# A two-layer decoder step on one core: three expert slots in turn through the whole loop, an early read of the overflow flag, and layer 1's keys transposed ahead of the last sums

## The reference

```python
group = argmax(hf @ wg + bg)                      # 4 groups
top_val, top_idx = top_k(exp_logits[group], 2)    # 2 of 8 experts in the group
gate = p_group * softmax(top_val)
for each of 32 experts e, on the rows that chose it:
    gu = xb @ w_up[e]                             # 1024 -> 2 x 512
    rows = (silu(gu[:, :512]) * gu[:, 512:]) @ w_down[e]
y[token] += rows * gate
```

## Time and profile before

| | |
|---|---|
| time, median of 3 runs | 1537.93 us (1533.36 to 1538.13) |
| profiled execution, its own time | 1538.02 us |
| its span, first to last instruction | 1536.4 us |
| mean granted TensorE clock | 0.957 |
| busy: PE / PEld / DVE / ACT / POOL | 1401.6 / 680.5 / 484.9 / 274.7 / 127.4 us |
| expert loop of layer 0 / of layer 1 | about 366 to 822 us / 1062 to 1518 us |
| read from HBM | 455.72 MB |

### The profile page before, as it was taken

How to read it: one execution, slowest core, us unless ns; L and a number is a source line. 1 busy time by engine, 2 the same in 40 slices (tenths; PEclk the granted TensorE clock), 3 DMA queues, 4 the chain that set the end, 5 groups by cost and what they waited for, 6 DMA issues and landing times.

```text
span 1536.4 us, 30978 instructions
## 1 busy us (share of the span) xinstructions
PE 1401.6 (91%) x13378; PEld 680.5 (44%) x13378; DVE 484.9 (32%) x1257; ACT 274.7 (18%) x748; POOL 127.4 (8%) x179
## 2 busy tenths in 40 slices
PE   7999998487999999999997599987999999999996
PEld 4477898344333333333333465744333333333332
DVE  3647375424122122122122425334122122122122
ACT  3214232201111111111112222110111111111111
POOL 3000586000000000000001010100000000000000
PEclk9999999798999999999998698998999999999998
DMA  9622300468799999999997345258799999999994
GB/s 338 192 83 48 78 4 4 120 274 328 317 396 428 426 430 429 429 428 428 429 426 246 116 103 173 95 203 358 318 392 428 427 428 428 430 429 427 427 428 179
DMA packets 69910, 463.63 MB, mean 302 GB/s; under 512 B 12002, under 2 KB 32732, under 8 KB 45052
## 3 DMA queue, kind: packets, MB, share of 16 engines
q1 hardware_dynamic: 68172, 456.00, 73.2%
q0 software_dynamic: 1648, 6.33, 1.5%
HBM read 455.72 MB, written 6.59 MB: 301 GB/s over the span
## 4 chain that ended last, share of the span: by engine, by line
PE 88%; DVE 7%; ACT 2%; issue 2%; POOL 0%; DMA 0%; POOLq 0%; DVEq 0%; SPq 0%; ACTq 0%
PE bank L1208 31%; PE bank L1194 12%; PE bank L751 10%; PE bank L1221 8%; PE bank L993 6%; PE bank L1272 4%; PE bank L910 4%; PE bank L1055 2%; PE bank L1201 2%; DVE arena L1773 2%; PE bank L928 1%; PE bank L801 1%; PE bank L897 1%; PE bank L721 1%; PE bank L860 1%
## 5 line engine op out<-in xcount | busy, mean ns | idle before, releaser
L1208 PE MATMUL bank<-slot,arena 128*32 128x256 f32 x3968 | 477.7, 631 | 1.0 <-DVE arena L1776 1.0
L1208 PEld LDWEIGHTS bank<-slot,arena 128*32 128x32 f32 x3968 | 137.7, 123 | 268.4 <-issue 252.9
L1194 PE MATMUL bank<-h,arena 128*32 128x256 f32 x1536 | 190.8, 640 | 1.2 <-DVE arena L1769 1.2
L1781 DVE SCALAR_TENSOR_TENSOR arena<-arena,bank 128x128 f32<-128x128 f32 x64 | 18.5, 289 | 366.7 <-ACT arena L1404 365.0
L1221 PE MATMUL bank<-slot,arena 128*32 128x256 f32 x1984 | 119.9, 382 | 0.7 <-ACT arena L1408 0.7
L1417 ACT COPY arena<-bank 32x256 f32<-32x256 f32 x252 | 91.4, 363 | 152.9 <-PE bank L1221 150.7
L1194 PEld LDWEIGHTS bank<-h,arena 128*32 128x32 f32 x1536 | 63.4, 129 | 113.2 <-issue 111.8
L1404 ACT ACTIVATE arena<-bank 128x128 f32<-128x128 f32 x64 | 17.8, 278 | 452.8 <-PE bank L1208 452.8
L565 POOL TENSOR_SCALAR arena<-arena 128x1 f32<-128x1 f32 (+2 forms) x18 | 5.8, 320 | 1054.6 <-ACT h L1392 1014.4
L2172 DVE TENSOR_TENSOR x<-bank,x 128x512 f32<-128x512 f32 x64 | 44.1, 691 | 138.3 <-PE bank L1272 138.0
L1272 PE MATMUL bank<-arena 128*128 128x512 f32 x128 | 73.6, 663 | 6.0 <-issue 6.0
(11 more groups left out here) (399 smaller groups left out, 1415.2 us busy)
## 6 DMA issues: line engine op xcount, KB each, us to landing
slot<-in_exp_w_up SPq DMA_DIRECT2D x124, 2048.0 KB, 15.9
slot<-in_exp_w_down SPq DMA_DIRECT2D x62, 2048.0 KB, 16.1
slot<-in_w_in SPq DMA_DIRECT2D x6, 1536.0 KB, 7.4
slot<-in_w_out SPq DMA_DIRECT2D x4, 2048.0 KB, 8.7
arena<-in_exp_w_up SPq DMA_DIRECT2D x2, 4096.0 KB, 26.8
slot<-in_w_in SPq DMA_DIRECT2D x3, 2048.0 KB, 8.1
slot<-in_w_in SPq DMA_DIRECT2D x5, 1024.0 KB, 11.1
slot<-in_w_mem_kv SPq DMA_DIRECT2D x2, 2048.0 KB, 13.6
```

The lines of the kernel that those rows point to most:

```text
L1194: last = pe.matmul(ps[0][strip * CAP:(strip + 1) * CAP, 0:DW], G[:, t, :], h[:, t, :].rearrange("p (f k) -> p k f", k=KT)[:, strip * (DW / ...
L1208: last = pe.matmul(ps[bank][strip * CAP:(strip + 1) * CAP, 0:2 * FW], xs[:, c, strip_k * CAP:(strip_k + 1) * CAP], up_cols(wup[slot_j], k, ...
```

## The change

Experts use the three slots in turn through the whole loop: expert e goes to slot e mod 3, and its load waits for expert e - 3. Since four experts make a quad and three slots a turn, TensorE's loop body becomes three quads (12 experts), run twice; VectorE's and ScalarE's loops stay at one quad, SP's takes three experts. The down part of the third slot is two DMAs. PE, ACT and DVE read the overflow flag behind the first quad; the `If` stays behind the last. TensorE transposes layer 1's keys behind the `If` of layer 0 and ahead of the last sums. Expert 30 is now in slot 0 and expert 31 in slot 1, so KC is loaded when expert 30 is done, then the two chunks when expert 31's up part is done, then VC. `select(1)` moves behind the norm's scales, since its place belongs to the third slot until then.

```diff
+RING = 3
+LOADS = [len(range(j, NE, RING)) for j in range(RING)]
@@ load_down
-            sp.dma_start(wdn[sl], A["exp_w_down"][l, bass.ds(e, 1)].rearrange("e (p k) n -> p (e k) n", p=128)).then_inc(sem, 16)
+            w = A["exp_w_down"][l, bass.ds(e, 1)].rearrange("e (p k) n -> p (e k) n", p=128)
+            if sl < THIRD:
+                sp.dma_start(wdn[sl], w).then_inc(sem, 16)
+            else:
+                for u in range(2):
+                    sp.dma_start(wdn_third[u], w[:, 2 * u:2 * u + 2, :]).then_inc(sem, 16)
@@ SP
+            def load_cache(l, name, to, sem):
+                for m in range(2):
+                    sp.dma_start(to[:, m], A[name][l].rearrange("b (m p) h d -> m p b (h d)", p=128)[m]).then_inc(s[sem], 16)
...
-                refill(3, 0, 0)
-                refill(4, 1, 1)
-                with sp.Fori(2, NE // 2 - 1) as i:
-                    refill(2 * i + 1, 0, 2 * i - 1)
-                    refill(2 * i + 2, 1, 2 * i)
-                refill(NE - 1, 0, NE - 3)
+                with sp.Fori(1, NE // RING) as i:
+                    for j in range(RING):
+                        refill(RING * i + j, j, RING * i + j - RING)
+                for e in range(NE // RING * RING, NE):
+                    refill(e, e % RING, e - RING)
                 if l == 0:
                     sp.wait_ge(s["m_used"], UNITS * (NE - 1))
+                    load_cache(1, "cache_mem_k", KC, "cache_k")
+                    sp.wait_ge(s["m_used"], UNITS * (NE - 1) + UNITS_UP)
                     for n in range(2):
                         load_w_in(1, n)
+                    load_cache(1, "cache_mem_v", VC, "cache_v")
@@ POOL
                 norm_scale(2 * l + 2)
-                if l == 0:
-                    pool.wait_ge(s["m_used"], UNITS * 3)
-                    select(1).then_inc(s["consts"], 1)
...
                 norm_scale(2 * l + 3)
+                if l == 0:
+                    select(1).then_inc(s["consts"], 1)
@@ PE
                 if l == 0:
                     memory0()
-                else:
-                    keys_T(1)
                 attention(l)
...
-                expert(0, 0, 0, loads[0] + 16, started=l > 0)
-                expert(1, 1, 1, loads[1] + 16, started=l > 0)
-                expert(2, THIRD, 0, 16 * (l + 1), between=places_between(0, l == 0))
-                expert(3, 0, 1, loads[0] + 32)
-                with pe.Fori(1, QUADS - 1) as g:
-                    expert(4 * g, 1, 0, loads[1] + 32 * g, between=sum_between(g - 1))
-                    expert(4 * g + 1, 0, 1, loads[0] + 32 * g + 16)
-                    expert(4 * g + 2, 1, 0, loads[1] + 32 * g + 16, between=places_between(g))
-                    expert(4 * g + 3, 0, 1, loads[0] + 32 * g + 32)
-                g = QUADS - 1
...
+                def quad(g, c, turn, places_first=False, sums=True, final=False):
+                    for j in range(4):
+                        sl = (c + j) % RING
+                        between = lambda k: None
+                        if j == 0 and sums:
+                            between = sum_between(g - 1)
+                        if j == 2:
+                            between = places_between(g, places_first)
+                        expert(4 * g + j, sl, j % 2, 16 * (LOADS[sl] * l + 1) + 16 * (turn + (c + j) // RING),
+                               started=sums or j >= 2 or l > 0, final=final and j == 3, between=between)
+                quad(0, 0, 0, places_first=l == 0, sums=False)
                 pe.wait_ge(s["flag"], l + 1)
                 more = pe.value_load(flag_i[0:1, 0:1], min_val=0, max_val=1)
+                with pe.Fori(0, 2) as i:
+                    for n in range(3):
+                        quad(3 * i + n + 1, 4 * (n + 1), 4 * i)
+                quad(QUADS - 1, 4 * (QUADS - 1), 0, final=True)
                 r = lambda n: s[f"r_{n}{l}"]
                 with pe.If(more > 0):
...
                 with pe.Else():
                     pe.nop()
+                if l == 0:
+                    keys_T(1)
                 pe.wait_ge(s["m_S4T"], QUADS * (l + 1))
@@ ACT, and DVE alike
                 quad(0, first=l == 0)
+                act.wait_ge(s["flag"], l + 1)
+                more = act.value_load(flag_i[0:1, 0:1], min_val=0, max_val=1)
                 with act.Fori(1, QUADS - 1) as g:
                     quad(g)
                 quad(QUADS - 1, final=True)
-                act.wait_ge(s["flag"], l + 1)
-                more = act.value_load(flag_i[0:1, 0:1], min_val=0, max_val=1)
```

More of the change, by code:

```diff
@@ L424, in _ @@
                     sp.dma_start(ga2[0:16, :], A["gla_a2"][0]).then_inc(s["lora_in"], 16)
-                for m in range(2):
-                    sp.dma_start(KC[:, m], A["cache_mem_k"][l].rearrange("b (m p) h d -> m p b (h d)", p=128)[m]).then_inc(s["cache_k"], 16)
-                    sp.dma_start(VC[:, m], A["cache_mem_v"][l].rearrange("b (m p) h d -> m p b (h d)", p=128)[m]).then_inc(s["cache_v"], 16)
+                if l == 0:
+                    load_cache(0, "cache_mem_k", KC, "cache_k")
+                    load_cache(0, "cache_mem_v", VC, "cache_v")
                 if l == 0:
@@ L466, in _ @@
                 load_down(sp, 1, 1, l, s["wdn1"])
-                sp.dma_start(wdn_third[1], third_down[:, 2:4, :]).then_inc(s["wdn_third"], 16)
+                sp.dma_start(wdn_third[1], third_down[:, 2:4, :]).then_inc(s["wdn2"], 16)
                 sp.wait_ge(s["norm_h"], 6 * (l + 1))
@@ L471, in _ @@
                 sp.wait_ge(s["logit_ps"], 3 * (l + 1))
-                sp.dma_start(wdn_third[0], third_down[:, 0:2, :]).then_inc(s["wdn_third"], 16)
+                sp.dma_start(wdn_third[0], third_down[:, 0:2, :]).then_inc(s["wdn2"], 16)
                 def refill(e, j, after):
@@ L496, in _ @@
                     sp.wait_ge(s["m_used"], UNITS * NE * (l + 1))
-                    load_up(sp, 0, 0, l, (s[f"rw{l}"],) * 2)
-                    load_down(sp, 0, 0, l, s[f"rw{l}"])
+                    load_up(sp, 0, THIRD, l, (s[f"rw{l}"],) * 2)
+                    load_down(sp, 0, THIRD, l, s[f"rw{l}"])
                     with sp.Fori(1, NE) as e:
                         sp.wait_ge(s[f"r_pe{l}"], len(REST["pe"]) * STEPS_REST * e)
-                        load_up(sp, e, 0, l, (s[f"rw{l}"],) * 2)
-                        load_down(sp, e, 0, l, s[f"rw{l}"])
+                        load_up(sp, e, THIRD, l, (s[f"rw{l}"],) * 2)
+                        load_down(sp, e, THIRD, l, s[f"rw{l}"])
                 with sp.Else():
@@ L1304, in expert @@
                     for k in range(KT):
[L1305 to L1307 removed]
+                        if k % (KT // 2) == 0:
                             pe.wait_ge(s[f"wup{'ab'[k // (KT // 2)]}{sl}"], loaded)
@@ L1321, in expert @@
                         pe.wait_ge(s["m_nat"], it - 1)
-                    if sl == THIRD:
-                        pe.wait_ge(s["wdn_third"], 2 * loaded)
-                    else:
-                        pe.wait_ge(s[f"wdn{sl}"], loaded)
+                    pe.wait_ge(s[f"wdn{sl}"], 2 * loaded if sl == THIRD else loaded)
                     for f in range(FF // 128):
                         down_f(sl, f, 6 + par).then_inc(s["m_used"], 1)
-                loads = [16 * (NE // 2) * l, 16 * (NE // 2 - 1) * l]
@@ L1339, in _ @@
-                g = QUADS - 1
-                expert(4 * g, 1, 0, loads[1] + 32 * g, between=sum_between(g - 1))
-                expert(4 * g + 1, 0, 1, loads[0] + 32 * g + 16)
-                expert(4 * g + 2, 1, 0, loads[1] + 32 * g + 16, between=places_between(g))
-                expert(4 * g + 3, 0, 1, loads[0] + 32 * g + 32, final=True)
+                def quad(g, c, turn, places_first=False, sums=True, final=False):
[8 more added lines that the diff above has]
+                               started=sums or j >= 2 or l > 0, final=final and j == 3, between=between)
@@ L1349, in _ @@
                     with pe.Fori(0, NE) as e:
-                        pe.wait_ge(s[f"rw{l}"], 48 * (e + 1))
+                        pe.wait_ge(s[f"rw{l}"], 64 * (e + 1))
                         for b in range(STEPS_REST):
@@ L1359, in _ @@
                             for k in range(KT):
-                                last = up_k(0, k, 2)
+                                last = up_k(THIRD, k, 2)
                             last.then_inc(r("pe"), 1)
@@ L1365, in _ @@
                             for f in range(FF // 128):
-                                last = down_f(0, f, 6)
+                                last = down_f(THIRD, f, 6)
                             last.then_inc(r("pe"), 1)
@@ L2205, in _ @@
                 quad(0, first=True)
+                dve.wait_ge(s["flag"], l + 1)
+                more = dve.value_load(flag_i[0:1, 0:1], min_val=0, max_val=1)
                 with dve.Fori(1, QUADS - 1) as g:
@@ L2212, in _ @@
                 last.then_inc(s["m_nat_dve"], 1)
-                dve.wait_ge(s["flag"], l + 1)
```

(1 more changed line is left out.)

7 lines of the change are left out of this document (2 added, 5 removed).

## The result

The changed kernel takes 1549.86 us (median of 7 runs, 1546.71 to 1555.79), the kernel before 1537.93 us beside it: a ratio of 1.0087, interval 1.0063 to 1.0111. The forecast was 1541.8 us in a range of 1534 to 1547: it had the sign, and a third of the size. By the prediction's own bounds this is slower, to which it gave 0.42.

What follows compares the result with a forecast made beforehand. The prediction took TensorE's pace to bound the expert loops. Flag -0.9 - 0.7 + 0.4, keys -2.0 and two jumps back +7.0 gave +3.8 us on 1538.0, so 1541.8 us, range 1534 to 1547.

Steps and rivals of the forecast that it cites:

- The bound and the third slot: Expert loops: they run at TensorE's pace with weights in time, so a third buffer removes no wait; gain 0.
- three quads aren't held: TensorE's jump from loop end to head: three quads of code exceed what the engine holds, so it takes 3.54 us.
- The price of the edge: One taken jump back in each layer's TensorE loop: 3.5 us, +7.0 for two, bounds 0 to 14.6.
- The second fetch: Behind the loop's jump back: a second instruction packet may be waited for, 0 to 3.5 us, taken as 0.3.
- the clock's term: TensorE behind the loop's jump back: 0.6 us, chosen between 0 and 1.2.
- The jump in layer 0: Jump past the overflow part, ahead of the last sums: it stays, at 3.54 us, and TensorE waits for it.
- The flag: Flag read leaves the loop's end: -0.9 and -0.7 us; at its new place behind the fourth expert +0.4 in all.
- The keys: Layer 0's end, keys transposed ahead of the last sums: -2.0 us, bounds -2.6 and -1.0.
- the second: Loop's jump back waits for two fetches and for the clock, 14.6 us in all: 1549.4 us; chance 0.08.
- Rival 1: Loop's jump back stays free, its code held or fetched ahead: not slower, 1534.8 us; chance 0.17.
- rival 3: Expert loops: weights are the bound after all and deeper loading lets TensorE run closer: 1534.1 us; chance 0.06.
- rival 4: Flag and keys gain nothing, being hidden already; only jumps back and new reads count: 1545.4 us; chance 0.09.

Runs made afterwards that it cites:

- numbers 4: Kernel before with only TensorE's loop body grown to three quads, run twice, with two slots and loads as they were: 1551.85 us, ratio 1.0089.
- 11: Kernel before with early flag, keys ahead, TensorE's overflow body as a loop (short jump), layer 1's two projection loads behind the jump: 1526.91 us, ratio 0.9945.
- number 2: Changed kernel with layer 1's first loads held back until TensorE's key transposes, behind its jump past the overflow part: 1545.41 us, ratio 1.0063.
- number 3: Changed kernel with weight refills cut to 128 KB a half, so most experts compute with old weights: one run of 1553.63 us.
- number 1: Changed kernel with TensorE's six inner quads written out, so that it jumps back nowhere: 1535.93 us, ratio 0.9994.
- experiment 5: Kernel before with only the flag read early and layer 1's keys transposed ahead of the last sums: 1532.88 us, ratio 0.9967.
- number 8: Kernel before with TensorE's loop body of two quads, run three times a layer, buffers and loads as before: one run of 1561.13 us.
- number 6: Changed kernel with TensorE's inner quads written out and layer 1's first loads issued behind the jump past the overflow part: 1531.94 us, ratio 0.9952.
- number 7: The kernel of number 6 with TensorE's overflow body as a loop over its eight steps, so the jump past it is short: 1527.54 us, ratio 0.9929.
- numbers 9: Changed kernel with a prefetch hint for the back edge's target at the head of each turn of TensorE's loop: 1549.49 us, ratio 1.0092.
- 10: Changed kernel with the back edge's prefetch hint behind the first up unit of the turn's last expert: 1550.72 us, ratio 1.0080.

## Why the prediction was wrong

Right in kind, wrong in one price, and blind to one side effect. Its steps:

- **The bound and the third slot: as forecast, 0.** Plain quads stay at 57.3 us, and numbers 4 and 11 show the slot to cost and bring nothing that can be measured.
- **That three quads aren't held, so that an edge waits: as forecast.** One wait in each layer, a packet beside it.
- **The price of the edge: the step that failed.** Its sum was 3.5 us an edge, and 7.16 and 6.66 us were measured, so 13.8 in place of 7.0. Its first term, 2.6 us of idle time, was taken from the jump of the earlier trace rows; 5.0 us were measured. Of its parts the branch failed, 6.05 us in place of 3.54; from its end to the first matmul it is 0.30 us (0.26 in the sum), and the lead was 1.35 (1.2). The jump of the earlier trace rows stood where the queue was empty, in layer 1 (DMA share 0.00 in 1516.9:1517.9), or running out: in layer 0 the DMA share is 0.93 over the first us behind the branch and 0.68 over the first 2.5. There the packet starts 1.0 to 1.1 us behind the branch. In the loop the DMA share is 1.0 throughout, which the prediction itself read in the earlier trace rows, and the packet starts 3.6 us behind it. Experiments 2 and 3 show it from both sides: without loads the jump is short again, and with small weight loads the quad over the edge is 3.9 and 4.1 us longer, near the sum's 3.5. The second fetch, put at 0.3 us within 0 to 3.5, was waited for: 1.46 and 0.98 us. No run shows the clock's term of 0.6 us, a choice between 0 and the 1.2 us by which four sums at layer 0's end (3.47 us) exceed twice 1.12 us; at the edges the two sums took 0.43 and 0.49 us more, the granted clock at 0.50. The prediction saw the full queue, but only as a risk to the second packet, not to the first. Its bounds for two edges, 0 to 14.6 us, hold the 13.8; its range of times, up to 1547, was drawn narrower.
- **The jump in layer 0: left out.** "The jump stays" was right for its instructions and not for its price. Layer 1's w_in chunks and cached values now load while it waits (the cached keys have landed by 825.5), and it grew by 3.1 us. The early loads were costed only at those who use them, and there the forecast held: the second chunk landed at 835.4, ahead of the projection at 849.16. What the change won at that place, 0.9 us for the flag and 1.3 for the keys, is less than that; so the changed kernel without its edges (number 1) is no faster than before.
- **The flag: as forecast.** Down matmuls to sums in layer 1: 4.08 us, against 4.88, -0.8; nothing clear lost at the new place (0.4 was allowed). For layer 0 number 2 shows it, where the jump is as before: 3.95 us from the down matmuls to the keys, against 5.02 to the sums before, with jumps of 3.42 and 3.53.
- **The keys: as forecast in kind.** The sums' tail is 2.2 us shorter and the transposes 0.9 us ahead of it, -1.3 in place of -2.0. The transposes and the first four sums ran at a granted clock of 0.50 behind the longer pause (window 833.40:837.90); with the short pause of number 2 the same rows give -2.1.
- **What is left.** Between layer 1's projection and its first gather 1.3 us were won, around the sample tokens' scores, where VectorE's wait fell from 9.0 to 6.6 us. Which of the moved parts did it was not tried.

The span grew by 11.8 us: edges +13.8, jump +3.1, other quads +0.5, flag -1.7, keys -1.3, scores -1.3, front -0.8, the rest of the last tail -0.5.

Of the rivals, the second came within half a microsecond of the time (1549.4), and only half of its reason holds: two packets are waited for, but the second costs 1.0 to 1.5 us rather than 3.5, and what makes up the difference is the first one's wait, and the jump, which it didn't have; that it came so near is luck in part. Rival 1 is out by the branch of 6.05 us and experiment 1, rival 3 by the plain quads, which didn't shrink, rival 4 by experiment 5. By its own splits the prediction's chances add up to 0.07 for faster, 0.52 for no change and 0.41 for slower; it wrote 0.08, 0.50 and 0.42.

One quad has 511 matmuls and as many weight loads, two quads some 2090 instructions with the sequencer's. The one-quad loop takes edges of 0.21 us without a fetch; in the two-quad loop of number 8 no edge is below 5.9 us. By the four packets of a quad in straight code, an estimate, about four packets of code are held and about eight aren't. A branch to code that isn't held took 3.3 to 6.7 us in these traces.

## What to carry to other kernels

Before a loop body of TensorE grows or a large part is written into a branch that isn't taken, count its instructions: a jump to code that isn't held stopped the engine for 1.93 us (number 6) to 5.66 us (number 8) here, and if it must be, it should fall where no large load is on its way. Take the price of such a stop from a place with the same DMA load, not from the nearest example. And a load moved to an earlier time can slow an instruction that has nothing to do with its data.

## What the runs showed of the hardware

- The packet that a branch waits for, 16 KB, mostly takes 1.0 to 1.1 us (0.9 to 1.4; 2.05 and 2.10 at the edges of number 3, with two under way). What varies is its start behind the branch: 0.9 to 1.2 us on a quiet queue (once 1.5; DMA share 0.00 behind the jumps of numbers 2 and 6 in layer 0), 3.4 to 4.3 us with weight or cache loads in flight all the while (share 1.01 behind the changed kernel's first edge, 1.08 behind its jump in layer 0). The branch ends 1.3 to 1.6 us after the packet's end. What in the DMA engines holds the packet back isn't shown.
- A high DMA share at the branch alone doesn't tell: with w_in's last bytes on their way (0.93 over the first us, then falling) the packet started 1.06 us behind the jump in the kernel before, and 1.57 us in number 5, where the share fell more slowly.
- A taken jump to code that is held costs 0.2 to 0.4 us in these traces (the one-quad loop's edges 0.21, number 7's short jumps 0.34 and 0.39).
- After 5.00 us of idle TensorE the granted clock was 0.50 for 3.4 us, 599.0 to 602.4 in the changed kernel; after 3.67 us, at the edge of number 3, it stayed at 1.00. But ahead of layer 0's last sums it fell to 0.50 after 3.09 us (before, window 826:828), 2.02 (number 2, window 830.1:833.3) and 1.93 us (number 6, window 823.3:826.7). So the length of the idle time alone doesn't decide; what does is open.
- A prefetch hint changed nothing at either place: the edges' branches took 6.06 to 6.13 us with it (numbers 9 and 10) and 6.05 without.
